# x kept in SBUF, the norms moved into the following stages, and an output projection that works chunk by chunk

## The reference

```python
def _rms_norm(x, w):
    return x * lax.rsqrt(jnp.mean(x * x, axis=-1, keepdims=True) + EPS) * w
def _modulate(h, shift, scale): return h * (1.0 + scale) + shift
def _gated_head_norm(o, gate, w):
    return o * lax.rsqrt(jnp.mean(o * o, axis=-1, keepdims=True) + EPS) * w * jax.nn.silu(gate)
for l in range(DEPTH):                       # DEPTH = 2
    h = _modulate(_rms_norm(x, norm1_w[l]), sh1, sc1)
    # even: HGRN2 mixer, 8 heads of 128; odd: GLA mixer, 4 heads of 256
    o = scan(h @ w_in); m = _gated_head_norm(o, og, gnorm_w) @ w_out
    x = x + g1 * m
    h = _modulate(_rms_norm(x, norm2_w[l]), sh2, sc2)
    x = x + g2 * _peer(h, w_q[l], keys[l], u[l], v[l])     # experts by product keys
y = _rms_norm(x, final_norm_w)
```

## Time and profile before

| | |
|---|---|
| median of 3 runs | 4770.8 us (4769.79 to 4777.8) |
| the profiled execution | 4781.13 us, its span 4779.4 us |
| mean granted clock of TensorE | 0.932 |
| busy: TensorE, VectorE, ScalarE, GpSimd | 87%, 80%, 35%, 40% |
| moved | 1075.63 MB, 225 GB/s |

### The profile page before, as it was taken

The page is one execution under the profiler, slowest core; times in us unless marked ns, Lnnn a source line. Parts: engine busy times, 40 slices in busy tenths (PEclk is TensorE's granted clock), DMA queues, the critical chain, the costliest instruction groups (busy, mean ns, idle before and its releaser), DMA issues. The chain is left out here.

```text
span 4779.4 us, 72684 instructions
## 1 busy us (share of the span) xinstructions
PE 4149.2 (87%) x24365; PEld 3725.2 (78%) x24365; DVE 3831.5 (80%) x6663; ACT 1689.4 (35%) x2360; POOL 1921.0 (40%) x1414
## 2 busy tenths in 40 slices
PE   7689994696899999999986888666789999999996
PEld 3489883684799999999975877566679999999995
DVE  7488886289888888999985776449988888899995
ACT  7544442221333333333324433231333333333332
POOL 0033431122654545566642221211544544566661
PEclk9799996897999999999997988888899999999998
DMA  9411111220999999999981110221499999999995
GB/s 372 146 47 53 45 41 59 86 60 21 252 369 362 362 362 357 363 364 361 363 314 52 51 39 19 96 77 30 109 306 362 362 362 361 358 364 360 363 361 212
DMA packets 622024, 1075.63 MB, mean 225 GB/s; under 512 B 230324, under 2 KB 389495, under 8 KB 621175
## 3 DMA queue, kind: packets, MB, share of 16 engines
q1 hardware_dynamic: 473814, 535.07, 33.0%
q0 software_dynamic: 147456, 536.94, 30.2%
q10 hardware_dynamic: 672, 2.62, 0.2%
HBM read 1001.10 MB, written 73.40 MB: 225 GB/s over the span
## 5 line engine op out<-in xcount | busy, mean ns | idle before, releaser
L1823 POOL DMA_INDIRECT rows_ex<-in_peer_v,ctx_index x512 | 707.2, 1381 | 476.5 <-DVE row_acc_ex L1893 360.9
L1823 POOL DMA_INDIRECT rows_ex<-in_peer_u,ctx_index x512 | 586.6, 1146 | 631.5 <-DVE dots_ex L1896 504.4
L1983 PE MATMUL pu_ex<-h_hi,uT_hi_ex 128*128 128x384 f32 x2048 | 714.8, 349 | 1.9 <-ACT coef_ex L1843 1.0
L1893 DVE SCALAR_TENSOR_TENSOR row_acc_ex<-rows_ex,factor_ex,row_acc_ex 128x1024 f32<-128x1024 f32 x512 | 657.8, 1285 | 52.9 <-issue 11.2
L1983 PE MATMUL pu_ex<-h_lo,uT_hi_ex 128*128 128x384 f32 x2048 | 691.6, 338 | 0.0
L1983 PE MATMUL pu_ex<-h_hi,uT_lo_ex 128*128 128x384 f32 x2048 | 691.1, 337 | 0.0
L1991 PE MATMUL py_ex<-v_hi_ex,c_hi_ex 128*128 128x512 f32 x1536 | 622.8, 405 | 0.0
L1896 DVE CUSTOM_DVE_ANT_0 rows_ex<-rows_ex,h_row_ex 128x1024 f32<-128x1024 f32 x512 | 604.7, 1219 | 0.0
L1991 PE MATMUL py_ex<-v_hi_ex,c_lo_ex 128*128 128x512 f32 x1536 | 604.1, 393 | 0.0
L1991 PE MATMUL py_ex<-v_lo_ex,c_hi_ex 128*128 128x512 f32 x1536 | 601.2, 391 | 0.0
L1832 ACT ACTIVATE uT_hi_ex<-pT_ex 128x512 fp32r<-128x512 f32 x512 | 304.3, 594 | 562.1 <-PE pT_ex L1976 506.8
(11 more groups left out here) (362 smaller groups left out, 8576.4 us busy)
## 6 DMA issues: line engine op xcount, KB each, us to landing
u_raw_ex<-in_peer_u SPq DMA_DIRECT2D x256, 512.0 KB, 6.9
v_raw_ex<-in_peer_v SPq DMA_DIRECT2D x256, 512.0 KB, 6.2
ada<-in_ada_w SPq DMA_DIRECT2D x24, 2048.0 KB, 11.8
gates<-stage_ro SPq DMA_DIRECT2D x12, 4096.0 KB, 16.0
g_raw_ex<-gates SPq DMA_DIRECT2D x256, 192.0 KB, 6.2
w_raw_hgrn<-in_hgrn_w_in SPq DMA_DIRECT2D x40, 512.0 KB, 4.4
w_raw_re<-in_peer_w_q SPq DMA_DIRECT2D x32, 512.0 KB, 4.1
w_raw_gla<-in_gla_w_in SPq DMA_DIRECT2D x25, 512.0 KB, 4.2
```

What stands on the lines that cost most here:

```text
L1823: pool.indirect_dma_start(out=rows[m % RING][:, :], out_offset=None, in_=a["peer_u" if m < TG * NC else "peer_v"].rearrange("l n d -> (l n ...
L1893: nc.vector.scalar_tensor_tensor(row_acc[g][:, :], rows[j][:, :], factor[:, j:j + 1], row_acc[g][:, :], ALU.mult, ALU.add).then_inc(row_fr ...
L1983: last_ = nc.tensor.matmul(pu[:, 0:TD], w[:, k, :], x[:, k, 0:TD], start=(k == 0 and w is uT_hi[b] and x is h_hi), stop=(k == DC - 1 and w ...
```

## The change

1. `x`, `acc` (128x640) and `inv` (128x40) are tiles of the whole program. x is no longer reloaded by norm, experts and finish; the mixer puts its output `oT` in x's place, so setup and experts still store x once (`x_saved`, awaited by ScalarE in the mixer) and mix_out reads it back. To make room, `posf`, `m`, `s4`, `s2` in route share their space with two of its ring buffers.
2. Whoever makes x last also sums its squares into `acc`: ScalarE squares, and GpSimd (setup, experts) or VectorE (mix_out) adds.
3. The stage `norm` is gone. A class `Norm` gives each engine its piece inside mixer and retrieve: TensorE turns `acc` into row sums, tokens on the partitions, 128x1 for each of NT = 5 tiles of tokens; VectorE and ScalarE invert five columns; TensorE spreads them over all partitions by five matmuls with the identity. The scaled chunk takes one instruction of VectorE (two parts), the shift is ScalarE's bias. In odd chunks ScalarE writes the shifted value back to `y` and copies it to `h_hi`, and GpSimd makes `h_lo`; in even chunks ScalarE writes `h_hi` at once, and VectorE makes `h_lo` from y + shift. `y` is three deep. `first_product` does six matmuls for each chunk as it becomes ready; in the HGRN mixer it is the first of the two late products, so two weights are split during the norm.
4. mix_out sums squares in the same way (ScalarE even, VectorE odd chunks), inverts all heads at once (40 columns in layer 0), spreads head by head into one PSUM buffer (`spread_s`, `spread_c`), and does the first AHEAD = 3 output chunks chunk by chunk: 18 matmuls a chunk. The other five follow as whole products. Weight buffers are three deep.
5. finish scales on the way out of PSUM, through four tiles and two engines, and stores five tiles of 512 KB.

The squares in setup (the same three lines stand at the end of experts), the class `Norm`, and how mixer uses it on GpSimd, ScalarE and TensorE; retrieve uses it in the same way, and there both weights are split:

```diff
+            for k in range(1, DC):
+                pool.wait_ge(squared, k + 1)
+                pool.tensor_tensor(c["acc"][:, :], c["acc"][:, :], sq[k % 2][:, :], ALU.add)
+                pool.drain().then_inc(gathered, 1)
...
+            def square(k):
+                if k >= 3:
+                    act.wait_ge(gathered, k - 2)
+                act.activation(sq[k % 2][:, :] if k else c["acc"][:, :], xT[:, k, :], ACT.Square).then_inc(squared, 1)
...
+class Norm:
...
+    def tensor(self, pe):
+        nc, c = self.nc, self.c
+        for t in range(NT):
+            last = nc.tensor.matmul(self.rows[:, t:t + 1], c["acc"][:, t * P:(t + 1) * P], c["ones_d"][:, 0:1],
+                                    start=True, stop=True)
+        last.then_inc(self.summed, 1)
+        pe.wait_ge(self.rooted, 1)
+        for t in range(NT):
+            last = nc.tensor.matmul(self.spread[t], self.inv[:, t:t + 1].to_broadcast([P, P]), c["ident"][:, :],
+                                    start=True, stop=True)
+        last.then_inc(self.spread_done, 1)
+    def root(self, act):
+        act.wait_ge(self.inverted, 1)
+        act.activation(self.inv, self.inv, ACT.Sqrt).then_inc(self.rooted, 1)
+    def high(self, act, k):
+        act.wait_ge(self.y_done, k + 1)
+        dst = self.y[k % 3][:, :] if k % 2 else self.h_hi[:, k, :]
+        for v, cols in parts():
+            last = act.activation(dst[:, cols], self.y[k % 3][:, cols], ACT.Identity,
+                                  bias=self.c["mod"][:, self.layer, self.sh + k, v:v + 1])
+        if k % 2:
+            act.drain()
+            last = act.activation(self.h_hi[:, k, :], self.y[k % 3][:, :], ACT.Copy)
+        last.then_inc(self.hi_done, 1)
+    def low_odd(self, pool, k):
+        pool.wait_ge(self.hi_done, k + 1)
+        pool.tensor_tensor(self.h_lo[:, k, :], self.y[k % 3][:, :], self.h_hi[:, k, :].bitcast(F32), ALU.subtract) \
+            .then_inc(self.lo_done[1], 1)
+    def vector(self, dve):
...
+        dve.wait_ge(self.spread_done, 1)
+        def scaled(k):
+            if k >= 3:
+                dve.wait_ge(self.lo_done[(k - 3) % 2], (k - 3) // 2 + 1)
+            for v, cols in parts():
+                last = nc.vector.scalar_tensor_tensor(self.y[k % 3][:, cols], c["x"][:, k, cols],
+                                                      c["scale_w"][:, k, v:v + 1], self.by[v], ALU.mult, ALU.mult)
+            last.then_inc(self.y_done, 1)
+        def low(k):
+            dve.wait_ge(self.hi_done, k + 1)
+            for v, cols in parts():
+                last = nc.vector.scalar_tensor_tensor(self.h_lo[:, k, cols], self.y[k % 3][:, cols],
+                                                      c["mod"][:, self.layer, self.sh + k, v:v + 1],
+                                                      self.h_hi[:, k, cols].bitcast(F32), ALU.add, ALU.subtract)
+            last.then_inc(self.lo_done[0], 1)
+        scaled(0)
+        for k in range(DC):
+            if k + 1 < DC:
+                scaled(k + 1)
+            if k % 2 == 0:
+                low(k)
+def first_product(nc, pe, nm, psum, w_hi, w_lo, proj):
+    for k in range(DC):
+        pe.wait_ge(nm.lo_done[k % 2], k // 2 + 1)
+        for i, cols in halves():
+            for n, (w, x) in enumerate(((w_hi, nm.h_hi), (w_hi, nm.h_lo), (w_lo, nm.h_hi))):
+                last = nc.tensor.matmul(psum[i][:, 0:HALF], w[:, k, :], x[:, k, cols], start=(k == 0 and n == 0),
+                                        stop=(k == DC - 1 and n == 2))
+            if k == DC - 1:
+                last.then_inc(proj, 1)
...
+                lo(-1, L)
+            for k in range(1, DC, 2):
+                nm.low_odd(pool, k)
+                if k == 3 and not mx.gla:
+                    lo(-1, L + 1)
...
+                hi(-1, L)
+            for k in range(DC):
+                nm.high(act, k)
+                if k == 2 and not mx.gla:
+                    hi(-1, L + 1)
...
+            nm.tensor(pe)
+            pe.wait_ge(w_lo_done, 1)
+            first_product(nc, pe, nm, pp, w_hi[L % 2 if PRE == 0 else 0], w_lo[L % 2 if PRE == 0 else 0], proj)
```

mix_out, by SyncE, GpSimd, ScalarE, TensorE and VectorE in turn:

```diff
+            gates(0)
+            weights(0)
+            weights(1)
+            gates(1)
+            weights(2)
+            gates(2)
+            gates(3)
+            sp.dma_start(x[:, :, :], x_sp).then_inc(x_in, 16)
+            for j in range(AHEAD, DC):
+                sp.wait_ge(w_lo_done, j - AHEAD + 1)
+                weights(j)
...
+                gate(k)
+                if k < AHEAD:
+                    low(k)
+            for j in range(AHEAD, DC):
+                low(j)
...
+            act.wait_ge(inverted, 1)
+            act.activation(inv, inv, ACT.Sqrt).then_inc(rooted, 1)
+            sigmoid(0)
+            high(0)
+            high(1)
+            sigmoid(1)
+            high(2)
+            for k in range(DC):
+                if k + 2 < DC:
+                    sigmoid(k + 2)
+                act.wait_ge(y_done, k + 1)
+                act.activation(h_hi[:, k, :], y[k % 3][:, :], ACT.Copy).then_inc(hi_done, 1)
...
+            for g in range(H):
+                for k in range(g * NV, (g + 1) * NV):
+                    pe.wait_ge((sq_act, sq_dve)[k % 2], k // 2 + 1)
+                for t in range(NT):
+                    for k in range(g * NV, (g + 1) * NV):
+                        last = nc.tensor.matmul(rows[:, g * NT + t:g * NT + t + 1], sq[k % 2][:, t * P:(t + 1) * P],
+                                                c["ones_d"][:, 0:1], start=(k % NV == 0), stop=(k % NV == NV - 1))
+                last.then_inc(summed, NV)
+            pe.wait_ge(rooted, 1)
+            def spread(g):
+                if g:
+                    pe.wait_ge(spread_read, g)
+                for t in range(NT):
+                    dst = spread_s[:, t, :] if t < NT - 1 else spread_c[:, :]
+                    last = nc.tensor.matmul(dst, inv[:, g * NT + t:g * NT + t + 1].to_broadcast([P, P]),
+                                            c["ident"][:, :], start=True, stop=True)
+                last.then_inc(spread_done, 1)
...
+            spread(0)
             for k in range(DC):
+                if k % NV == NV - 1 and k // NV + 1 < H:
+                    spread(k // NV + 1)
+                if k == 0:
+                    pe.wait_ge(w_lo_done, AHEAD)
+                pe.wait_ge(lo_done, k + 1)
+                for j in range(AHEAD):
+                    for i, cols in halves():
+                        last = terms(j, k, i, cols)
+                        if k == DC - 1:
+                            last.then_inc(proj, 1)
+            for j in range(AHEAD, DC):
+                pe.wait_ge(w_lo_done, j + 1)
                 for i, cols in halves():
+                    pe.wait_ge(added, 2 * (j - AHEAD) + i + 1)
+                    for k in range(DC):
+                        last = terms(j, k, i, cols)
+                    last.then_inc(proj, 1)
...
+            def normal(k):
+                g = k // NV
+                dve.wait_ge(spread_done, g + 1)
+                by = (spread_s[:, :, :].rearrange("p t n -> p (t n)"), spread_c[:, :])
+                for v, cols in parts():
+                    last = nc.vector.scalar_tensor_tensor(y[k % 3][:, cols], oT[:, k, cols],
+                                                          c["vec"][:, gw + k % NV:gw + k % NV + 1], by[v],
+                                                          ALU.mult, ALU.mult)
+                if k % NV == NV - 1:
+                    last.then_inc(spread_read, 1)
+            def low(k):
                 dve.wait_ge(hi_done, k + 1)
-                nc.vector.tensor_sub(h_lo[:, k, :], y[k % 2][:, :], h_hi[:, k, :].bitcast(F32))
+                nc.vector.tensor_sub(h_lo[:, k, :], y[k % 3][:, :], h_hi[:, k, :].bitcast(F32)).then_inc(lo_done, 1)
+            for k in range(DC):
+                normal(k)
+                dve.wait_ge(gate_done, k + 1)
+                dve.drain()
+                nc.vector.tensor_mul(y[k % 3][:, :], y[k % 3][:, :], og[:, k, :]).then_inc(y_done, 1)
+                if k >= 1:
+                    low(k - 1)
+            low(DC - 1)
```

The store of x at the end of experts, and the transposes and scaled copies in finish:

```diff
-            sp.dma_start(xT[:, :, :], x_sp).then_inc(x_in, 16)
-            for k in range(DC):
-                sp.wait_ge(x_added, k + 1)
-                sp.dma_start(x_sp[:, k, :], xT[:, k, :]).then_inc(x_out, 16)
-            sp.wait_ge(x_out, 16 * DC)
+            if layer + 1 < DEPTH:
+                sp.wait_ge(x_added, DC)
+                sp.dma_start(x_sp, xT[:, :, :]).then_inc(x_saved, 16)
...
+            pe.wait_ge(weighed, DC)
+            for n in range(2 * NT):
+                if n >= 4:
+                    pe.wait_ge((out_a, out_d)[n % 2], (n - 4) // 2 + 1)
+                for k in range(4):
+                    last = nc.tensor.transpose(pt[n % 4][:, k, :], x[:, 4 * (n % 2) + k, n // 2 * P:(n // 2 + 1) * P],
+                                               c["ident"][:, :])
```

(9 more changed lines are left out.)

486 lines of the change are left out of this document (208 added, 278 removed).

## The result

The changed kernel takes 4646.48 us (median of 4 runs, 4644.8 to 4650.44); the kernel before, on the same chip, 4770.98 (4 runs, 4769.79 to 4777.8). The ratio is 0.9737, 95% interval 0.9721 to 0.9754. It is faster by 124.5 us; forecast were 185, and the range ended at 4630. The direction was right; the gain was a third smaller than forecast.

The account below looks back on a forecast made before the run. Experts loops were taken as bound by TensorE and DMA and untouched; gains lay in chains where stages meet. 32.9 + 33.8 + 29.5 + 34.8 + 18.4 + 11.2 + 27.5 - 3 = 185 us, giving 4586 from 4770.8, range 4562 to 4630.

Parts of the forecast that it names:

- The norms: Four norms with the first product behind each: gains of 32.9, 33.8, 29.5 and 34.8 us.
- the three pairs of 4.1: In a norm, the first three pairs of chunks take 4.1 us each, before 3.1 for the last pair.
- the lock: VectorE's two-input instructions wait out GpSimd's; as rival, at every meeting: +22 us, 4608, chance 0.15.
- Setup: GpSimd's seven additions meet VectorE's two-input subtractions in setup: 0 to 7 us, taken as a loss of 3.
- Output projection: Both layers' mix_out: 115.8 and 103.6 us, gains 18.4 and 11.2; spread, VectorE and matmuls in series, 7.1 us a chunk.
- Eight row sums of 1.2 with one square ahead, 10.5: Start of the output projection: TensorE's row sums take 10.5 us, at 0.12 us a record.
- 4.3 + 7.1: Layer 0's output projection: 4.3 us for the first chunk's 18 matmuls, partly at half clock, then 7.1 a chunk.
- GpSimd's sum 5.6 us behind the last x: Behind the experts, GpSimd's additions of squares, 7 x 1.62 us, end 5.6 us after the last x.
- list of seven places: Where the change acts: four norms with the first product behind each, two output projections, the finish.
- experts' transfers lose rate: Slower rival in the experts loops: tiles move within SBUF, DMA has no slack; 10% less rate gives 4824 us; chance 0.02.
- The clock rival: In the projection's chunk loop TensorE falls to 1.2 GHz, 3.3 us more a period: 4625 us; chance 0.15.
- Free overlap: Rival for the projection: spreads don't hold TensorE, 3.3 us less in six periods, about 10 in layer 1: 4556; chance 0.06.

Follow-up runs that it names:

- e6: Changed kernel with VectorE instead of GpSimd making the norms' low parts of odd chunks, GpSimd only those of the weights: 4646.66 us, ratio 0.9731.
- e2: Changed kernel with one GpSimd drain added in experts, behind the indirect transfers and ahead of the additions of squares: 4630.39 us, ratio 0.9703.
- e10: Changed kernel with one GpSimd drain at the very start of its program in experts, ahead of the indirect transfers: 4646.34 us, one run.
- e1: Changed kernel with the tile inv 64 values wide instead of 40, so every tile behind it starts 96 bytes later: 4625.27 us, ratio 0.9690.
- e4: Changed kernel with mix_out's first three weights loaded ahead of the gates, split ahead of the root, low parts made during the row sums: 4634.88 us, ratio 0.9713.
- e3: Changed kernel with VectorE in mix_out making chunk k's low part right behind its gate, ahead of the next chunk's scaling: 4619.04 us, ratio 0.9678.
- e5: Changed kernel with the tile inv 48 values wide, route's stage tiles starting 192 bytes past a multiple of 512: 4652.03 us, one run.
- e7: Changed kernel with four buffers instead of two for the squares of the mixer's output in mix_out: 4643.46 us, ratio 0.9725.
- e8: Changed kernel with e1, e2, e3, e4 and e7 together, the first early weight split put between two squares: 4566.36 us, ratio 0.9565.

## Why the prediction was wrong

- **The norms: right**, in mechanism and in the sum. 24.9 us to the end of HGRN's first product (25.1 forecast), 29.0 and 28.9 from the last x to retrieve's (27.9), a lock that stretches one or two instructions a norm. That the sum came out to 0.2 us is in part luck: ScalarE's first chunk began at 6.7 us for 5.6, the rest behind the fourth pair's start took 6.0 for 7.2, and the three pairs of 4.1 were pairs of 3.0, 3.6 and 5.6. That it was right on the lock was no proof that GpSimd's share pays; e6 shows that it neither pays nor costs.
- **Setup: right**, -2.7 for -3. VectorE's subtractions took 5.2 us in place of 4.42 beside the additions, as it said.
- **Output projection: the mechanism right, two terms mis-sized.** The period was 6.77 us for 7.1 (and 10.48 for 10.13 a pair in layer 1). "Eight row sums of 1.2 with one square ahead, 10.5" failed: 15.4 us in layer 0, 21.5 in layer 1. The 0.12 us a record is a price of clock 1.00. It held for 2.94 us (0.11 measured); then the clock fell to 0.50, and a record took 0.213. The prediction named the double price at 1.2 GHz for the norm's row sums and left it out here. The second term is the same 10.5 in layer 1: there the squares have two buffers for a head's two chunks, so that TensorE waits three times 1.01 us for the next pair, and all 80 records were at the lower clock. The prediction had named the record's price as its weak point (0.25 would cost 10 us) but kept the low end of it. The first matmul came 3.8 us late in layer 0 and 9.8 in layer 1, which is nearly all of layer 1's miss of 10.1. In layer 0 another 2.4 of the 6.0 us are the first two chunks (from 760.95 to the spread at 774.73, 13.8 us for 4.3 + 7.1), mostly at clock 0.50.
- **Experts to the next stage: one term missing.** "GpSimd's sum 5.6 us behind the last x" was 13.4, in the finish 13.1 for 5.4. The 7.4 us are the first drain behind the transfers (e2 and e10), a term that the sum "7 x 1.62 us" doesn't have. The trace of before had a sign of it, the drain of 17.0 us at the end of the stage, but there it stood in the shadow of TensorE's last products and delayed nothing. The rest of these stretches was 2 to 2.5 us better than forecast.
- **Route: not looked at at all.** The prediction's list of seven places holds none in route or experts. Of the experts loops it says that the change leaves them alone; route it puts at nothing without a reason. The change puts three tiles ahead of the tiles of all stages, of 20,480, 2560 and 160 bytes in each partition, and the 160 moved what lies behind them off its alignment. All 18.5 us came back with 96 bytes of padding, and some 3 more, since route without waits for stores is shorter than before (e1). The rival "experts' transfers lose rate" looked in that direction, at the wrong stage and with a reason (tiles move within SBUF) that it did not follow to an address.
- **The rivals.** The clock rival came half true: the row sums and the first matmuls ran at 0.50, but ahead of the loop and not in it. In the chunk loop of the changed kernel the clock fell to 1.2 GHz for 3.4 us in layer 0 and not at all in layer 1, and the period was 6.77 us, not 10; with the earlier start of e4 it did fall, three times in layer 1. "Free overlap" was not what happened, and e3 shows what it would have been worth, with one line moved: 27.4 us, for some 30 by the prediction's terms. The range reached up to the clock rival alone, and held no case for a cost in a stage without an edit of its own.

## What to carry to other kernels

Behind a small tile that isn't a multiple of the length of a transfer's pieces, every other tile moves: compare the start addresses of all tiles that DMA moves in short pieces, and the landing times of every transfer, also in stages that the edit doesn't touch. When a producer's order on one engine is written "next chunk first, then finish this one", look whether the next chunk waits for something that stands behind this one on another engine; moving one line was worth 27 us here. Price short matmuls at the clock that the stretch will have, not at that of the row they are read from.

## What the runs showed of the hardware

- A DMA of 4 MB in pieces of 256 bytes took 15.9 to 16.0 us from SBUF tiles that start at a multiple of 256 bytes, and 23.2 to 23.3 us from tiles that start 160 or 192 bytes past one (e1, e5).
- The first GpSimd drain behind 512 indirect transfers delayed the next addition by 7.4 us, after 22 us without work; the next ones cost 0.2 to 0.5 (changed kernel, e10). Right behind the transfers such a drain took 10.1 us (e2).
- The lock between VectorE and GpSimd works both ways: 1.53 us became 5.5 for an addition of GpSimd beside VectorE's 128x4096 subtractions, 1.01 became 3.61 for VectorE beside GpSimd's 128x1024. A scaling with one input in PSUM was not held (1.91 us for two chunks beside GpSimd, 1.92 without).
- A matmul with one column cost 0.11 us a record (two records each) at granted clock 1.00, and 0.213 at 0.50, with gaps around it or without (changed kernel, e7, e8).
- The clock fell from 1.00 to 0.50 while TensorE did such row sums without a pause, 2.94 us after an idle time of 2.04 (layer 0, at 732.9).
